# Start, latent queries, modulation units and output projection of a two-layer trunk step rearranged together

## What is computed

```python
def _layer(x, cond, p, lam_init, pos, ctx):
    mod = jnp.einsum('bd,de->be', jax.nn.silu(cond), p['w_ada']) + p['b_ada']
    sh1, sc1, g1, sh2, sc2, g2 = jnp.split(mod[:, None, :], 6, axis=-1)
    h = _rms(x, p['g_norm1']) * (1 + sc1) + sh1
    u = h @ p['w_in']
    gates, xa, qkv_da, xc, mla_in = jnp.split(u, IN_SPLITS, axis=-1)
    ...
    q = (_rms(c_q, p['mla_qa_norm']) @ p['w_uq']).reshape(B, T, MLA_HEADS, MLA_QK)
    ckv_n = _rms(c_kv, p['mla_kv_norm'])
    ...
    proj = jnp.einsum('btnw,nwd->btnd', branches, p['w_branch'])
    merged = jnp.sum(gsig * proj, axis=2)
    x = x + g1 * (merged @ p['w_out'])
    h2 = _rms(x, p['g_norm2']) * (1 + sc2) + sh2
    x = x + g2 * _conv_ffn(h2, p['w_up'], p['conv_w'], p['conv_b'], p['w_down'])
```

## Time and profile before

| | us |
|---|---|
| median of three runs (lowest, highest) | 1300.15 (1300.1, 1300.42) |
| the profiled execution | 1300.75 |
| its span, first to last instruction | 1299.0 |
| TensorE matmul busy | 1276.6 (98%) |
| VectorE / ScalarE / GpSimd busy | 778.1 / 593.4 / 86.1 |
| mean granted TensorE clock | 0.995 of 2.4 GHz |

### The profile page before, as it was taken

The page is one execution under the profiler, slowest core; times in us unless marked ns, Lnnn a source line. Parts: engine busy times, 40 slices in busy tenths (PEclk is TensorE's granted clock), DMA queues, the critical chain, the costliest instruction groups (busy, mean ns, idle before and its releaser), DMA issues.

```text
span 1299.0 us, 20279 instructions
## 1 busy us (share of the span) xinstructions
PE 1276.6 (98%) x8202; PEld 1183.4 (91%) x8202; DVE 778.1 (60%) x1480; ACT 593.4 (46%) x989; POOL 86.1 (7%) x73
## 2 busy tenths in 40 slices
PE   6999999999899999999999999999999999999999
PEld 5996988889889999999989888888899899999998
DVE  3544377446768777773353633864485787888432
ACT  3455454543355444442244564545433655455321
POOL 0000000004510000000010000000072000000000
PEclk8999999999999999999999999999998999999999
DMA  9551254443544444348553312434336233333333
GB/s 376 203 187 67 75 202 146 171 171 100 207 148 151 159 146 156 137 164 290 179 216 130 124 65 82 146 130 151 141 114 234 107 125 122 127 131 130 130 131 129
DMA packets 52686, 198.11 MB, mean 153 GB/s; under 512 B 6320, under 2 KB 6736, under 8 KB 51184
## 3 DMA queue, kind: packets, MB, share of 16 engines
q1 hardware_dynamic: 52272, 196.11, 42.0%
q0 software_dynamic: 320, 0.69, 0.2%
HBM read 194.51 MB, written 2.26 MB: 151 GB/s over the span
## 4 chain that ended last, share of the span: by engine, by line
PE 88%; DVE 5%; POOL 4%; ACT 1%; issue 1%; DMA 0%; SPq 0%; DVEq 0%; POOLq 0%; ACTq 0%
PE bank L1227 24%; PE bank L1229 24%; PE bank L1228 24%; PE bank L1185 2%; POOL merge_sum L504 2%; DVE w_lo L828 1%; PE bank L1478 1%; POOL wide L501 1%; POOL wide L502 1%; PE bank L1508 1%; PE bank L1298 1%; PE bank L1488 1%; PE bank L1299 1%; PE bank L1300 1%; DVE small L1045 1%
## 5 line engine op out<-in xcount | busy, mean ns | idle before, releaser
L1227 PE MATMUL bank<-act_hi,w_hi 128*128 128x384 f32 x1368 | 466.6, 341 | 1.4 <-DVE act_lo L872 1.2
L1229 PE MATMUL bank<-act_hi,w_lo 128*128 128x384 f32 x1368 | 457.9, 335 | 0.0
L1228 PE MATMUL bank<-act_lo,w_hi 128*128 128x384 f32 x1336 | 446.7, 334 | 0.0
L828 DVE TENSOR_TENSOR w_lo<-w_raw,w_hi 128x1024 fp32r<-128x1024 f32 x251 | 308.0, 1228 | 213.2 <-ACT w_hi L511 212.7
L511 ACT ACTIVATE w_hi<-w_raw 128x1024 fp32r<-128x1024 f32 x251 | 263.3, 1050 | 149.2 <-DMA w_raw<-stream 142.9
L1227 PEld LDWEIGHTS bank<-act_hi,w_hi 128*128 128x128 f32 x1368 | 257.3, 188 | 9.4 <-issue 7.8
L1229 PEld LDWEIGHTS bank<-act_hi,w_lo 128*128 128x128 f32 x1368 | 256.7, 188 | 0.0
L1228 PEld LDWEIGHTS bank<-act_lo,w_hi 128*128 128x128 f32 x1336 | 251.0, 188 | 1.2
L1227 PE MATMUL bank<-mlp_hi,w_hi 128*128 128x384 f32 x352 | 119.8, 340 | 0.0
L1228 PE MATMUL bank<-mlp_lo,w_hi 128*128 128x384 f32 x352 | 119.0, 338 | 0.0
L1229 PE MATMUL bank<-mlp_hi,w_lo 128*128 128x384 f32 x352 | 119.0, 338 | 0.0
(11 more groups left out here) (217 smaller groups left out, 1556.4 us busy)
## 6 DMA issues: line engine op xcount, KB each, us to landing
w_raw<-stream SPq DMA_DIRECT2D x251, 512.0 KB, 3.2
ada<-ada_w SPq DMA_DIRECT2D x56, 512.0 KB, 3.7
start_ada<-start_ada SPq DMA_DIRECT2D x8, 1024.0 KB, 16.1
ada_norm<-ada_w SPq DMA_DIRECT2D x16, 512.0 KB, 5.9
ada_head_a<-ada_w SPq DMA_DIRECT2D x8, 512.0 KB, 5.9
time_consts<-time_consts SPq DMA_DIRECT2D x2, 1920.0 KB, 9.7
start_raw<-start_w SPq DMA_DIRECT2D x8, 448.0 KB, 17.2
params<-params SPq DMA_DIRECT2D x2, 926.0 KB, 12.5
```

Of the source, the lines that this page charges most:

```text
L828: V.tensor_tensor(wlo[s][:, :], raw[s][:, :], whi[s][:, :].bitcast(F32), ALU.subtract).then_inc(lo_ready, 1)
L1227: T.matmul(out, wb[s][0][:, w, :], hi[k], start=first and k == 0, stop=False)
L1228: T.matmul(out, wb[s][0][:, w, :], lo[k], start=False, stop=False)
L1229: ins = T.matmul(out, wb[s][1][:, w, :], hi[k], start=False, stop=last and k == n - 1)
```

## The change

1. Start. VectorE adds the squares of blocks 4h, 4h + 1 to those of 4h + 2, 4h + 3; TensorE sums four blocks instead of eight, behind eight products of ones with ones that need only the matrix of ones. The wait for the conditioning moves behind the sums. `start_low(0)` and `start_high(0)` move behind the first `wide` and behind the reciprocal root.
2. Latent queries. The sum of c_kv goes first, then c_q; the norms follow in that order; the four 128-row matmuls go ahead of the four 64-row ones.
3. Modulation units run in pairs in attention, up and down projection; the down projection's tiles are loaded in pairs.
4. Branches. Four sets of gated tiles (two of them over `act_lo`); GpSimd adds two tiles of 384 in one instruction of 768, then the rest; the splits of output units 1 and 2 move ahead of the last gating, later ones are one unit further ahead, and the extra split in front of the second norm goes; `pair` is gone, `group` takes three output units, the third two blocks behind the others.

```diff
+WARM = 8
-ADA_STEP = ([2, 2, 1, 1, 1, 1, 0] + [1] * 8 + [0] + [1] * 8, [1, 0] * 8 + [1] * 8)
+ADA_STEP = ([2, 2, 0, 2, 0, 2, 0] + [0, 2] * 4 + [0] + [2, 0] * 4, [2, 0, 0, 0] * 4 + [2, 0] * 4)
-OUT_BANK = (2, 5, 0, 1)
+OUT_BANK = (2, 5, 4, 0)
+SUM_BANK = (4, 3)
+GATED = 4
+        late_t, _ = tile("gated_late", KD * TOK, o)
...
-        gated = wide_t[:, :].rearrange("p (a n t) -> p a n t", a=2, n=4)
+        gated = [wide[:, 0:4, :], wide[:, 4:8, :], late[:, 0:4, :], late[:, 4:8, :]]
...
-                        if n % 3 == 2 and n < 18:
+                        if n in (5, 11, 17):
                             load_ada(ring)
-                            ring += 1
+                            load_ada(ring + 1)
+                            ring += 2
...
-                    own(nc.gpsimd.tensor_tensor(gated[:, s, 0, :], gated[:, s, 0, :], gated[:, s, 1, :], ALU.add))
-                    own(nc.gpsimd.tensor_tensor(gated[:, s, 2, :], gated[:, s, 2, :], gated[:, s, 3, :], ALU.add))
+                    own(nc.gpsimd.tensor_tensor(g[:, 0:2, :], g[:, 0:2, :], g[:, 2:4, :], ALU.add))
                     own.wait()
-                    nc.gpsimd.tensor_tensor(msum[:, d % 4, :], gated[:, s, 0, :], gated[:, s, 2, :], ALU.add).then_inc(merged_ready, 1)
+                    nc.gpsimd.tensor_tensor(msum[:, d % 4, :], g[:, 0, :], g[:, 1, :], ALU.add).then_inc(merged_ready, 1)
...
-                            if k >= 1:
-                                start_high(k)
+                            start_high(k)
                             act.wait_ge(start_shift, k + 1)
...
+                split(B0 + 3)
                 for d in range(KD + 1):
-                    if 1 <= d < KD:
-                        split(B0 + d + 2)
+                    if 1 <= d < KD - 1:
+                        split(B0 + d + 3)
+                    if d == KD - 2:
+                        split(O0 + 2)
                     if d >= 1:
                         act.wait_ge(merged_ready, l * KD + d)
...
                         square(d - 3)
-                    split(O0 + d + 2)
+                    split(O0 + d + 3)
                 logs()
                 for k in (KD - 2, KD - 1):
                     act.wait_ge(x1_ready, FROM + l * KD + k + 1)
                     square(k, 1)
-                split(P0 + 2)
                 norm(1)
...
+                dve.wait_ge(start_sq_dve, h + 1)
+                dve.wait_ge(start_sq_act, h + 1)
+                V.tensor_tensor(wide[:, 4 * h:4 * h + 2, :], wide[:, 4 * h:4 * h + 2, :], wide[:, 4 * h + 2:4 * h + 4, :],
+                                ALU.add).then_inc(start_sq_sum, 1)
...
-                    if j == 0:
-                        start_low(0)
                     own.wait()
                     dve.wait_ge(rstd_ready, 1)
...
                     ins.then_inc(norm_full, 1)
-                    if j >= 1:
-                        start_low(j)
+                    start_low(j)
...
-                    if (d, n) == (KD - 1, 0):
-                        split(O0 + 1)
...
-                    if d >= 2:
-                        dve.wait_ge(merged_ready, l * KD + d - 1)
+                    if d >= GATED:
+                        dve.wait_ge(merged_ready, l * KD + d - GATED + 1)
...
                     if n == 3 and 1 <= d < KD - 1:
                         split(B0 + d + 2)
-                    if n == 3 and d >= 2:
-                        merged_low(d - 2)
-                merged_low(KD - 2)
-                merged_low(KD - 1)
+                        if d == KD - 2:
+                            split(O0 + 1)
+                        if d >= 2:
+                            merged_low(d - 2)
+                split(O0 + 2)
+                for d in range(KD - 3, KD):
+                    merged_low(d)
...
-                    split(O0 + d + 2)
+                    split(O0 + d + 3)
                     dve.wait_ge(unit_done, FROM + l * UNITS + O0 + d + 1)
...
-                split(P0 + 2)
                 norm(1)
...
-                def pair(u, banks, hi, lo, wait):
...
+                def group(u, banks, hi, lo, wait, lag=0):
+
+                    half = KD // 2
+                    outs = [bank[b][:, 0:TOK] for b in banks]
                     for k in range(KD):
                         wait(k)
                         for q in range(2):
-                            ins = dense(bank[banks[q]][:, 0:TOK], u + q, [k], hi[k:k + 1], lo[k:k + 1], k == 0, k == KD - 1)
+                            if k == 0:
+                                unit_ready(u + q)
+                            ins = dense(outs[q], u + q, [k], hi[k:k + 1], lo[k:k + 1], k == 0, k == KD - 1)
                             if k == KD - 1:
                                 ins.then_inc(unit_done, 1)
...
+                        at = k - lag
+                        if 0 <= at < half:
+                            if at == 0:
+                                unit_ready(u + 2)
+                            dense(outs[2], u + 2, [at], hi[at:at + 1], lo[at:at + 1], at == 0, False)
+                    dense(outs[2], u + 2, range(half, KD), hi[half:], lo[half:], first=False).then_inc(unit_done, 1)
...
-                    for k in range(KD):
-                        if k % 2 == 0:
-                            pe.wait_ge((start_sq_act, start_sq_dve)[k // 2 % 2], k // 4 + 1)
-                        ins = T.matmul(bank[4][:, 0:TOK], cc("ones"), wide[:, k, :], start=k == 0, stop=k == KD - 1)
+                    for _ in range(WARM):
+                        T.matmul(bank[6][:, 0:P], cc("ones"), cc("ones"), start=True, stop=True)
+                    for h in range(2):
+                        pe.wait_ge(start_sq_sum, h + 1)
+                        for k in (4 * h, 4 * h + 1):
+                            ins = T.matmul(bank[4][:, 0:TOK], cc("ones"), wide[:, k, :], start=k == 0, stop=k == 5)
...
                 for h in range(HEADS):
-                    out = bank[4 + h][0:QKW, 0:TOK]
-                    T.matmul(out, pc("w_uq_a", h * QKW, (h + 1) * QKW), pj[:, PJ["cq"], :], start=True, stop=False)
-                    T.matmul(out, pc("w_uq_b", h * QKW, (h + 1) * QKW, 0, NOPE), pj[0:NOPE, PJ["cqr"], :],
+                    T.matmul(bank[4 + h][0:QKW, 0:TOK], pc("w_uq_a", h * QKW, (h + 1) * QKW), pj[:, PJ["cq"], :],
+                             start=True, stop=False)
+                for h in range(HEADS):
+                    T.matmul(bank[4 + h][0:QKW, 0:TOK], pc("w_uq_b", h * QKW, (h + 1) * QKW, 0, NOPE), pj[0:NOPE, PJ["cqr"], :],
                              start=False, stop=True).then_inc(uq_done, 1)
...
-                pair(O0, OUT_BANK, MH, ML, lambda k: pe.wait_ge(mrg_lo, l * KD + k + 1))
+                group(O0, OUT_BANK[0:3], MH, ML, lambda k: pe.wait_ge(mrg_lo, l * KD + k + 1), lag=2)
...
-                    if l < DEPTH - 1 and 1 <= i < 1 + KD:
-                        ring_ada(UP_ADA + i - 1, UP_ADA + i)
+                    if l < DEPTH - 1 and i in (1, 3, 5, 7):
+                        ring_ada(UP_ADA + i - 1, UP_ADA + i + 1)
...
-                        if l < DEPTH - 1 and at < KD - 1:
-                            ring_ada(DOWN_ADA + at, DOWN_ADA + (KD if at == KD - 2 else at + 1))
+                        if l < DEPTH - 1 and at in (1, 3, 5, 6):
+                            pair = DOWN_ADA + 2 * (1, 3, 5, 6).index(at)
+                            ring_ada(pair, pair + 2)
```

51 lines of the change are left out of this document (19 added, 32 removed).

## The result

| | before | after |
|---|---|---|
| median of the runs, us | 1300.15 | 1288.97 (7 runs, 1287.12 to 1294.29) |
| profiled execution, us | 1300.75 | 1288.97 (span 1287.2) |
| ratio to the kernel before | | 0.9927, 95% interval 0.9913 to 0.9941 |

What follows compares the result with a forecast made beforehand. TensorE's own instruction issue was taken to bound the kernel, with few waits. Start 5.6, latent queries 2.3, paired units 4.6 and output projection 6.7 sum to 19.2 us off 1300.75: 1281.5, median 1281.0, range 1276.5 to 1288.5.

Steps and rivals of the forecast that it cites:

- the output projection: TensorE's 3.26 us stop on w_lo goes, part is given back before the second norm: 6.7 us over two layers.
- no longer waits for gating: In the output projection, GpSimd's last merge (d = 7) ends near 343.5, leaving 0.6 us of cover.
- I cost GpSimd at nothing: In the output projection, GpSimd's merges cost nothing; a merge held by the moved conversion would lose 0.3 us a layer.
- The wait ahead of the sums: Before the second norm, converting P0+2 ahead of the last residual delays the last sum: 1.4 us a layer given back.
- The start: Fewer sums of squares, an earlier first product and a faster first modulation round: 5.6 us, bounds 2.9 and 7.4.
- Round 0: First modulation round after the start: runs at the high clock level, about 4 us instead of 6.56, 2.7 us saved.
- Latent queries: Fewer changes of operand shape in the w_uq matmuls and the cq and ckv sums: 2.3 us, bounds 1.5 and 2.6.
- Paired units: Modulation units merged in attention (2.3 us) and up and down projection (2.3 us): 4.6 us, bounds 3.0 and 5.0.
- Rival 2: The new wait ahead of the second norm is long and drops the clock: 1291 us; chance with mixtures 0.13.
- Rival 1: The start stays cold and the first modulation round runs low as before: 1284 to 1286 us; chance 0.17.
- Rival 5: At the start, the ones do nothing and the sums gain little: 1283 us, inside the forecast, no separate chance.
- rival 4: Paired loads delay weight units in SyncE's queue, TensorE waits 1.7 us at each of 25 merges: 1323 us; chance 0.03.

Runs made afterwards that it cites:

- experiment 2: The kernel before with only the change's start part put in: 1296.29 us (7 runs), ratio 0.9973.
- experiment 8: The changed kernel without the eight products of ones: 1291.24 us in one execution, 1293.11 in six runs; beside each other 1290.57 without, 1288.72 with ones.

## Why the prediction missed

**The step that failed** is the output projection, "3.26 + 0.1, so 3.4 us a layer" with "1.05 to 2.25 of the 3.4 us are given back": forecast 6.7 us, measured 0.2 in the stages and nothing in the runs with the part undone. It has three faults.

- "Four gate buffers, the split one step earlier and a third unit in the group take that away." They moved it. The stop of 3.26 us became one of 2.27. I had asked whether GpSimd and merged_lo would be in time for k = 7, and not whether w_lo of the third unit would be there after three blocks. In VectorE's order it stands behind two conversions, a merged_lo and four gatings. Gain a layer: 0.9 instead of 3.4, with the longer spacings around the stop. The reading of the old stop was also half wrong: I had put it in part on VectorE's gating at d = 7, but the conversion stood ahead of that gating, and VectorE idled 1.12 us for ScalarE's high half, which was queued behind merged_hi (timelines of VectorE and ScalarE in the kernel before):

```profile
336.11 1.04 ACT L511 ACTIVATE w_hi<-w_raw 128x1024 fp32r<-128x1024 f32 x1
337.18 1.77 DVE L828 TENSOR_TENSOR w_lo<-w_raw,w_hi 128x1024 fp32r<-128x1024 f32 x1 [1.12 <-ACT w_hi L511]
338.87 0.54 DVE L1099 SCALAR_TENSOR_TENSOR wide<-gates_a,bank 128x384 f32<-128x384 f32 x1
```

Nor is it so that GpSimd's last merge "no longer waits for gating": in the changed kernel it waits 1.06 us for it, and with the third unit later the next wait was on merged_lo, 1.24 us.

- "I cost GpSimd at nothing." I had read GpSimd's delay by VectorE and not the reverse. Beside the new add of 768 columns a merged_lo took 2.20 us, and with adds of 384 it took 1.37. The Trainium skill, GPSIMD Engine Reference, section Specifications, names contention between the two engines for VectorE instructions with two SBUF inputs. I had set this against the forecast at 0.3 us a layer, on the merge; the trace agrees with the rule, but the price was on VectorE and 1.2 us of stop (2.27 to 1.05).
- The wait ahead of the sums was forecast in place and kind (ScalarE's squares, the conversion of P0+2 first), at 1.4 a layer; it was 1.9 and 1.7, since ScalarE's earlier square too was queued behind a conversion that waited for its transfer.

That makes for layer 0 -0.9 + 1.9 = +1.0, as seen. In layer 1 the clock fall is gone in this execution (2.7, as forecast), and a new wait of 0.41 us on w_hi at 982.66 costs 0.7 with the longer spacings around it: -0.9 - 2.7 + 0.7 + 1.7 = -1.2, as seen. The 2.7 is in part luck: behind the stop of 2.27 us the level fell in 9 of 20 cases.

**The start** was right and a little low: 5.6 forecast, 6.5 in the profile. Round 0 gave the 2.7 us as worked out, the first product came 3.8 us earlier (forecast 2.9 to 4.7). By itself the start is worth only 3.7 us, since more clock is lost behind the stops of the output projection with it (experiment 2).

**Latent queries**: 2.0 against 2.3, inside the bounds of 1.5 and 2.6.

**Paired units**: 4.6 forecast, 3.0 measured. Up projection as forecast (four merges of 0.33, 1.4 seen). Attention came near its sum because two errors cancelled. A merge is worth 0.19 us there and not 0.13 (8 merges in layer 1 gave 1.5; the 10 of layer 0 gave 1.9 with the units at their old steps), and the new place of the units cost 1.3, with the 0.81 us wait in it; I had written that "TensorE waits nowhere in attention now" (it did once, 0.28 us at the scores in layer 1) of the loads, and had asked of SyncE only, not what else the moved unit covered. The down projection lost 0.4 instead of gaining 1.0: the pairs took away the single unit that brings the closer spacing. None of the rows above the prediction shows it; to see it one must divide a stretch by its count, to four digits.

**The rivals.** None of them is what happened in the changed kernel's profile. Rival 2 is nearest, a wait in place of the one removed that drops the clock; but in 9 of 20 cases the fall came at the stop itself. Ahead of the norm, where I had looked for it, it came once, in experiment 8's single execution without ones (TensorE's timeline, and the granted clock behind the POOL column, 0.50):

```profile
365.97 0.98 PE L1262 MATMUL bank<-wide,consts 128*128 128x384 f32 x2 [2.38 <-POOL wide L485]
...
368.02 1.48 PE L1266 MATMUL bank<-wide,consts 128*128 128x384 f32 x2
```

```profile
368.00:370.00 2.00, 2.00 (x11) 0.67 (x13) 0.00 (x0) 0.46 (x1) 0.00 (x0) 0.50 0.49 195
```

Rival 1, a low round 0, was seen in part in the one execution with 5.4 us (experiment 8). Rival 5 is not settled: the ones probably do something, in under half of the executions profiled. For rival 4: no wait in attention is released by a load, so the paired loads cost nothing there.

## What to carry to other kernels

Where a stall on a converted weight is to go, write out the queue of the engine that converts, backwards and forwards from the stall, with durations beside their real neighbours: a stall that is "taken away" for one unit is moved to the next, unless that queue gets shorter. Before a small filler is moved or merged, ask what it covered, on every engine and not only on the queue that loads for it. And where a stop sometimes drops the clock, compare stages by executions that did not have the fall, since one of 2.7 us is as large as the things that one wants to measure; then look at the mean granted clock of all the runs, since a change can make the falls rarer or more frequent.

## What was not expected of the hardware

- Clock falls behind stops in the middle of dense work, counted over all profiled executions, both layers: behind stops of 3.26 us in 5 of 6 cases (9 to 17 products at 0.32 us), behind stops of 2.27 us in 9 of 20 (9 or 10 products, 1.5 us), behind waits of 1.24 us or less in 0 of 10. Ahead of the second norm it came behind one of four waits of 2.27 to 2.38 us. The same kernel has it or not from one execution to the next. It is a part of the spread of the changed kernel, 1286.9 to 1294.3: its runs below 1289 us have a mean granted clock of 1.000, the two slowest of the first seven 0.995 and 0.996.
- After eight matmuls of ones the level at 8 us is the high one in 5 of 12 executions, the low one in the others, at the same instructions, with the first sum starting within 0.3 us of the same time (8.04 to 8.31).
- Dense products have two spacings at a granted clock of 1.0, 0.1733 and 0.1768 us, over tens of microseconds, and a single 8-record unit of another shape changes from the longer to the shorter. 16 records in one go do not.
- A GpSimd add of 768 columns took 1.84 to 2.82 us, and beside the one of 2.82 VectorE's two-input instruction was four times as long (2.20 against 0.56 alone). Adds of 384 columns took 1.0 to 2.1, and beside them the same VectorE instruction took at most 1.37.
